# A fused two-block network: five FFN phases start on the unnormalised stream

## The chip, the cores and the metric

The kernel runs on one core of a Trainium2 chip, as one launch. The metric is the device time of that launch in microseconds (us). The core has five engines that matter here, each with a queue of its own that is worked off in order: TensorE (PE), VectorE (DVE), ScalarE (ACT), GpSimd (POOL) and SyncE (SP, which issues the weight loads). They are held together by semaphores alone.

## What is computed

A batch of one, 256 tokens, width 1024. Two networks of two layers each follow one another on the stream x. Cut to what matters:

```python
def rms_norm(x, g):
    return x * rsqrt(mean(x * x, axis=-1) + EPS) * g
def modulate(h, shift, scale):
    return h * (1 + scale) + shift

# first network, layers i = 0, 1 (nine vectors of 1024 from c_act @ ada_w[i] + ada_b[i])
h = modulate(rms_norm(x, ln_ffn1[i]), sh1, sc1)
x = x + 0.5 * g1 * swiglu(h, wg, wu, wd)          # phases F0, F2
h = modulate(rms_norm(x, ln_mix[i]), sh2, sc2)
x = x + g2 * mixer(h)                             # A (attention), G (spatial gating)
h = modulate(rms_norm(x, ln_ffn2[i]), sh3, sc3)
x = x + 0.5 * g3 * swiglu(h, wg, wu, wd)          # phases F1, F3
x = rms_norm(x, ln_out[i])

# second network, layers 0, 1 (six vectors each)
x = x + g1 * mixer(rmsnorm(x, norm_mix) * (1 + sc1) + sh1)     # H (HGRN2), N (sparse attention)
x = x + g2 * conv_ffn(rmsnorm(x, norm_ffn) * (1 + sc2) + sh2)  # C0, C1
# last: rmsnorm(x, final_norm)

swiglu(h, wg, wu, wd) = (silu(h @ wg) * (h @ wu)) @ wd          # hidden width 2816
conv_ffn: a, v = split(h @ w_up); a = three causal taps over the tokens + conv_b
          (silu(a) * v) @ w_down
```

## The kernel before

**Phases.** The order is F0, A, F1, F2, G, F3, H, C0, N, C1, then the last norm. The stream x lies in SBUF with the width on the partitions: eight blocks k of 128 channels, each 128 x 256 tokens. It is never turned around between phases.

**Slabs.** All weights stream from HBM in slabs of 128 x 2048 numbers of float32. Each slab is split for TensorE into a high part (`split_hi`, a cast on ScalarE, L1853) and a low part, raw minus high (`split_lo`, VectorE, L1986; at the border of two phases in two halves, L2001). A product with one slab is 48 matmuls of 256 columns: high x high, high x low and low x high, summed in PSUM (`three`, L1627 to L1629). TensorE waits for a slab's low part (`slab_ready`), and a split waits until TensorE has used the slab that lay in its buffer (`slab_used`). So the splits run two to four slabs ahead of TensorE, and where they stand in the ScalarE's and VectorE's queues is written out by hand.

**An FFN phase** with first slab b works on 11 chunks of 256 hidden channels. Chunk i takes three slabs: gate and up (`ups(i)` on TensorE, into PSUM `up`) and down (`down(i)`, into PSUM `dacc`). TensorE's order is ups(0), ups(1), down(0), ups(2), down(1), and then a loop over chunks 3 to 10. Between gate and down, ScalarE makes the Silu (L1909; in C0 and C1 first the tap part L1913, then two VectorE instructions for each half, L2141 and L2144, then the Silu L1919), VectorE the product with up (L2154), ScalarE its high part (L1924) and VectorE its low part (L2159). down(i) waits for the last of these.

**Modulation vectors.** In F0, F1, F2, F3 and C0 VectorE also multiplies tiles of the modulation matrix (`ada_tile`, 128 x 1024, L2021 and L2024), eight for one vector. TensorE then sums them over the partitions (`ada_sum`, L1721), the first time ahead of chunk 3. That sum stands in TensorE's queue, so a late eighth tile holds TensorE up. GpSimd issues the loads of these tiles.

**The norm at a phase's start** (`norm` on each engine). Behind the residual (L2119) ScalarE squares the eight blocks (L1871), GpSimd adds blocks 0 to 3 (`pre_add`, L1576), TensorE sums what is left over the partitions with a matrix of ones (`norm_sums`, five instructions in float32, recorded as ten, L1741) and then makes 24 dummy products whose result nobody reads (`keep_warm`, L1725 to L1729). ScalarE takes the root (L1877), VectorE the reciprocal (L2057), eight scalings x * a * (1/root) (L2060), ScalarE adds the shift and rounds to the high part of the operand (L1890, one per block) and VectorE makes the low part (L2064). TensorE's first product (`first_product`, L1652 and L1658) takes high parts block by block and then the low parts.

**Gained phases.** x = rms_norm(x, ln_out) behind F1 and F3 is not made before F2 and H, but folded into their norm: VectorE squares the plain x as well (`plain_squares`, L2111), GpSimd adds these eight too, TensorE sums them behind the first product (`gain_sum`), ScalarE takes the root (`row_kept`), and VectorE updates x itself (`gain_update`: a reciprocal and eight scalings), in F2 in halves around the slab b+3 and in H in its first two steps. In H GpSimd then builds masks, with fills and selects of 128 x 64 (L783 to L786).

Of the kernel before, what the change touches and what calls it, by code (L numbers as in the profile page):

```python
# [34 lines left out]
P = 128  # L35
# [65 lines left out]
def build(nc, T, out):  # L101
    phases = PHASES
    nslabs = sum(SLABS_OF.get(p, FFN_SLABS) for p in phases)
    with ExitStack() as ctx:
# [28 lines left out]
        work = sb("work", 12500)  # L133

# [6 lines left out]
        def op_k(t, k):  # L141
            return t[:, k * SEQ:(k + 1) * SEQ]

# [19 lines left out]
        table_col = small[:, 124:125]  # L163

# [5 lines left out]
        def bank(t, j):  # L170
            return t[:, j * 512:(j + 1) * 512]

# [13 lines left out]
            ada_step ada_summed mod_done x_turned squared squared_g presummed presummed_g sums_done sums_g_done  # L186
# [64 lines left out]
        gained = [phases[i + 1] for i, p in enumerate(phases) if p in OUT_COL]  # L251

# [41 lines left out]
        squares_g = view(4096, 6144)  # L294
# [150 lines left out]
        def pe_attention(pe, slab_ready, col_product, row_product, down_product, operand_stat, operand_mov, ada_sum, token_product):  # L445
# [76 lines left out]
        def act_attention(act, link, split_hi, split_hi_next, head_norm):  # L522
# [137 lines left out]
        def pe_gating(pe, slab_ready, col_product, row_product, down_product, operand_stat, operand_mov, ada_sum, token_product):  # L660
# [33 lines left out]
        def act_gating(act, link, split_hi, split_hi_next, head_norm):  # L694
# [82 lines left out]
        def hgrn_pool_masks(pool, link):  # L777
            pool.wait_ge(S["x_done"], x_before("H"))
# [28 lines left out]
        def pe_hgrn(pe, slab_ready, col_product, row_product, down_product, operand_stat, operand_mov, ada_sum, token_product):  # L807
            b = BASE["H"]
            for m in range(8):
                slab_ready(b + m)  # L810
                if m >= 6:
                    pe.wait_ge(S["sg_done"], 2 * (m - 5))
                col_product(b + m, ab_banks[m % 6], "H" if m == 0 else None)
            pe.wait_ge(S["sg_done"], 8)
# [67 lines left out]
        def act_hgrn(act, link, split_hi, split_hi_next, head_norm):  # L882
# [16 lines left out]
            for m in range(12):  # L899
                split_hi(b + m + 2)  # L900
                if 1 <= m <= 8:
                    take(m - 1)
                if m == 6:
# [42 lines left out]
        def dve_hgrn(dve, link, split_lo, ada_tile, mod_vector, residual, gain_update, head_norm):  # L946
# [155 lines left out]
        def pe_nsa(pe, slab_ready, col_product, row_product, down_product, operand_stat, operand_mov, ada_sum, token_product):  # L1102
# [111 lines left out]
        def act_nsa(act, link, split_hi, split_hi_next, head_norm):  # L1214
# [322 lines left out]
        def _(pool):  # L1537
# [733 lines left out]
```

## Time and profile before

| | us |
|---|---|
| three runs | 1977.41, 1980.89, 1980.24 |
| median | 1980.24 |
| the profiled execution | 1976.79 |
| its span | 1975.1 |

The profile is one execution. Over its span TensorE is busy for 1861.2 us (94%), VectorE for 1379.1 (70%), ScalarE for 859.1 (43%) and GpSimd for 263.5 (13%). The mean granted clock of TensorE is 0.957 of its full speed. TensorE's busy time counts the overlap of matmuls that follow each other as they are recorded, so its share says that it is the engine to watch, not that it never waits. Where it waits, a timeline row carries in brackets the idle time before it and what ended it. The page's other parts (DMA, 209 GB/s on the mean) do not bear on the change.

### The profile page before, as it was taken

What the parts mean: (1) busy time and instruction counts of PE and PEld (TensorE: products, weight loads), DVE (VectorE), ACT (ScalarE), POOL (GpSimd) and SP (SyncE); (2) the same over time, 40 slices, a digit from 0 to 9 for tenths busy, and PEclk for the clock granted to TensorE, in tenths of its full rate; (3) what the DMA queues carried; (4) which work ended last, traced back from release to release, by engine and by line L of the source; (5) the groups of instructions that cost most, each with busy time, mean ns of one, the idle gap of its engine ahead of it and who ended that gap; (6) DMA issues with size and microseconds to landing.
All of it is one profiled execution on the core that took longest, in us unless ns stands there. A gap on an engine that the chain in (4) does not pass through costs nothing.

```text
span 1975.1 us, 35516 instructions
## 1 busy us (share of the span) xinstructions
PE 1861.2 (94%) x14231; PEld 1786.2 (90%) x14231; DVE 1379.1 (70%) x1523; ACT 859.1 (43%) x1140; POOL 263.5 (13%) x429
## 2 busy tenths in 40 slices
PE   6999998799998999999999998779999998999998
PEld 6999996799998999988999987779999996689998
DVE  6677698576677866755677786757687856746555
ACT  3433454543334343444333454445344543645444
POOL 2311100011112111100111223720111110000000
PEclk9999998799999999988999998989999996999999
DMA  9988674168883988472888664035788792025551
GB/s 350 369 290 305 217 267 170 30 215 286 275 306 122 330 298 273 153 254 69 294 278 298 211 204 158 23 107 178 259 293 272 191 271 71 1 74 172 188 175 42
DMA packets 256950, 411.93 MB, mean 209 GB/s; under 512 B 22055, under 2 KB 200785, under 8 KB 256722
## 3 DMA queue, kind: packets, MB, share of 16 engines
q1 hardware_dynamic: 223914, 291.32, 45.3%
q0 software_dynamic: 32432, 119.04, 16.5%
q8 instruction: 70, 1.15, 0.2%
q14 instruction: 30, 0.25, 0.0%
q10 hardware_dynamic: 504, 0.18, 0.0%
HBM read 409.43 MB, written 2.63 MB: 209 GB/s over the span
## 4 chain that ended last, share of the span: by engine, by line
PE 80%; DVE 9%; ACT 3%; DMA 2%; issue 2%; POOL 2%; SPq 1%; DVEq 0%; ACTq 0%
PE up L1627 13%; PE up L1629 13%; PE up L1628 13%; PE dacc L1627 8%; PE dacc L1628 8%; PE dacc L1629 8%; PE dacc L1698 3%; PE misc L1721 3%; PE up L1652 2%; ACT hi L1853 1%; DVE lo L1986 1%; POOL work L1560 1%; DVE rstd_row L2057 1%; PE misc L1741 1%; DVE ada_acc L2024 1%
## 5 line engine op out<-in xcount | busy, mean ns | idle before, releaser
L1986 DVE TENSOR_TENSOR lo<-raw,hi 128x2048 fp32r<-128x2048 f32 (+1 forms) x256 | 581.0, 2271 | 332.3 <-ACT hi L1853 332.0
L1853 ACT CAST hi<-raw 128x2048 fp32r<-128x2048 f32 (+1 forms) x266 | 498.7, 1877 | 512.3 <-PE dacc L1629 253.1
L1627 PE MATMUL up<-operand_hi,hi 128*128 128x256 f32 x2176 | 621.1, 285 | 1.0 <-DVE work L2154 1.0
L1629 PE MATMUL up<-operand_hi,lo 128*128 128x256 f32 x2176 | 618.0, 284 | 0.0
L1628 PE MATMUL up<-operand_lo,hi 128*128 128x256 f32 x2176 | 618.0, 284 | 0.0
L1627 PEld LDWEIGHTS up<-operand_hi,hi 128*128 128x128 f32 x2176 | 419.9, 193 | 1.8 <-issue 1.7
L1628 PEld LDWEIGHTS up<-operand_lo,hi 128*128 128x128 f32 x2176 | 419.9, 193 | 0.6 <-issue 0.5
L1629 PEld LDWEIGHTS up<-operand_hi,lo 128*128 128x128 f32 x2176 | 419.7, 193 | 0.0
L1628 PE MATMUL dacc<-act_lo,hi 128*128 128x256 f32 x1056 | 298.8, 283 | 0.0
L1629 PE MATMUL dacc<-act_hi,lo 128*128 128x256 f32 x1056 | 298.4, 283 | 0.0
L1627 PE MATMUL dacc<-act_hi,hi 128*128 128x256 f32 x1056 | 296.5, 281 | 0.0
L2024 DVE SCALAR_TENSOR_TENSOR ada_acc<-ada,small,ada_acc 128x1024 f32<-128x1024 f32 x199 | 255.0, 1282 | 7.7 <-DMA ada<-in_ada_w_dram 3.5
L1423 POOL DMA_DIRECT2D ada<-in_ada_w_dram x224 | 118.9, 531 | 1001.1 <-DVE ada_acc L2024 611.6
L1627 PEld LDWEIGHTS dacc<-act_hi,hi 128*128 128x128 f32 x1056 | 200.8, 190 | 0.0
L1629 PEld LDWEIGHTS dacc<-act_hi,lo 128*128 128x128 f32 x1056 | 198.2, 188 | 0.0
L1628 PEld LDWEIGHTS dacc<-act_lo,hi 128*128 128x128 f32 x1056 | 197.9, 187 | 0.0
L1627 PE MATMUL dacc<-operand_hi,hi 128*128 128x256 f32 x464 | 136.4, 294 | 4.6 <-DVE operand_lo L758 2.2
L1628 PE MATMUL dacc<-operand_lo,hi 128*128 128x256 f32 x464 | 133.7, 288 | 0.0
L1629 PE MATMUL dacc<-operand_hi,lo 128*128 128x256 f32 x464 | 133.4, 288 | 0.0
L1576 POOL TENSOR_TENSOR work<-work 128x256 f32<-128x256 f32 x44 | 39.9, 908 | 617.7 <-ACT work L1871 615.9
L1909 ACT ACTIVATE work<-up 128x512 f32<-128x512 f32 x44 | 26.3, 598 | 183.0 <-PE up L1629 182.5
L1627 PEld LDWEIGHTS dacc<-operand_hi,hi 128*128 128x128 f32 x464 | 91.6, 197 | 6.9 <-DVE lo L1986 2.8
(364 smaller groups left out, 2481.7 us busy)
## 6 DMA issues: line engine op xcount, KB each, us to landing
ada<-in_ada_w_dram POOLq DMA_DIRECT2D x224, 512.0 KB, 5.9
raw<-in_ffn_wg_dram SPq DMA_DIRECT2D x88, 512.0 KB, 4.8
raw<-in_ffn_wu_dram SPq DMA_DIRECT2D x88, 512.0 KB, 5.3
raw<-in_ffn_wd_dram SPq DMA_DIRECT2D x88, 512.0 KB, 4.5
raw<-in_ffn_w_up_dram SPq DMA_DIRECT2D x88, 512.0 KB, 4.5
raw<-in_ffn_w_down_dram SPq DMA_DIRECT2D x46, 512.0 KB, 4.4
raw<-in_hg_w_in_dram SPq DMA_DIRECT2D x32, 512.0 KB, 5.0
raw<-in_attn_w_qkv_dram SPq DMA_DIRECT2D x24, 512.0 KB, 7.2
```

The lines of the kernel that those rows point to most:

```text
L1423: eng.dma_start(ada_place(m), ada_source(v, k) if source is None else source).then_inc((ada_first if v < 2 else ada_full)[m % ATILES], 16)
L1576: ins = pool.tensor_tensor(op_k(sq, 0), op_k(sq, 0), op_k(sq, k), ALU.add)
L1627: pe.matmul(o, stat[0], mov[0], start=start, stop=False, skip_group_check=True)
L1628: pe.matmul(o, stat[0], mov[1], start=False, stop=False, skip_group_check=True)
L1629: return pe.matmul(o, stat[1], mov[0], start=False, stop=stop, skip_group_check=True)
L1652: pe.matmul(dst[:, b * SEQ:(b + 1) * SEQ], sl[q][:, k * SEQ + b * P:k * SEQ + (b + 1) * P], op_k(operand_hi, k), start=(k == 0 and b == 0 ...
L1698: last = pe.matmul(bank(dacc, 2 * t + h), stat(part, kk, t), sl[q][:, kk * D + h * 512:kk * D + (h + 1) * 512], start=(start and kk == 0 a ...
L1721: last = pe.matmul(bank(misc, 1)[:, k:k + 1], acc_of(v)[:, k * P:(k + 1) * P], ones[:, 0:1], start=True, stop=True, skip_group_check=True)
L1853: last = act.copy(put(slab(hi, s, SPL)), take(slab(raw, s, RAW)))
L1909: act.activation(silu_sb, bank(up, 0), ACT.Silu).then_inc(S["silu_done"], 1)
L1986: last = dve.tensor_tensor(put(slab(lo, s, SPL)), take(slab(raw, s, RAW)), put(slab(hi, s, SPL)).bitcast(F32), ALU.subtract)
L2024: dve.scalar_tensor_tensor(acc, t, c, acc, ALU.mult, ALU.add).then_inc(S["ada_step"], 1)
```

## The change

All FFN phases but F0 are now in `raw_first` (F1, F2, F3, C0, C1). With a = gain * (1 + scale) for each channel, the operand of a product is x * a / root + shift. Since 1/root belongs to the token (the column), W @ (x*a) can be made first, multiplied by 1/root and the shift's product W @ shift added. That is done for the gate and the up product of chunk 0:

- ScalarE rounds x * a to `raw_hi` in pairs of blocks between the squares, behind a first instruction that puts two columns of the shift behind each block. VectorE makes the shift's rest and, among the residual's instructions, `raw_lo` = x * a - raw_hi. A block is 258 columns wide.
- TensorE makes `raw_products`: 32 matmuls with raw_hi, the sums (three instead of five, since GpSimd now adds blocks 0 to 5), 16 with raw_lo, and the whole up product, into four banks of `dacc`. The dummy products are gone in these phases. The products from chunk 1 on use the normed operand as before.
- VectorE copies the shift's column as a bias and multiplies with the root row (`first_scaled`), ScalarE's Silu takes the bias (`first_silu`; in C0 and C1 it makes the whole gate and then the tap part), and VectorE's `first_product` adds up's bias and multiplies. down(0), which writes into dacc, waits for `up_scaled`.
- The splits move: slab b+2 ahead of the root and the reciprocal, b+3 ahead of ScalarE's operand and behind VectorE's low parts, b+4 behind `first_silu` and `first_scaled` and ahead of the taps and the product.
- In F2 and H VectorE's eight plain squares are gone. GpSimd squares the plain blocks and adds them, 15 instructions. `gain_sum` stands behind ups(1) in F2 and behind the fourth product in H, the gain's root behind chunk 1 (H: step 5), and the update of x behind chunks 1 and 2 (H: steps 6 and 8). GpSimd's masks in H wait for the gain's sum. H keeps its norm otherwise.

```diff
 # POOL: pre_add
+top = 5 if name in raw_first else 3
+for k in range(1, top + 1):
+    ins = pool.tensor_tensor(op_k(squares, 0), op_k(squares, 0), op_k(squares, k), ALU.add)
+if name in gained:
+    pool.wait_ge(S["x_done"], x_before(name))
+    link(pool.tensor_tensor(gain_acc, op_k(x, 0), op_k(x, 0), ALU.mult))
+    for k in range(1, KB):
+        link(pool.tensor_tensor(gain_tmp, op_k(x, k), op_k(x, k), ALU.mult))
+        ins = pool.tensor_tensor(gain_acc, gain_acc, gain_tmp, ALU.add)
 # PE
+def raw_products(p):
+    slab_ready(b)
+    dst = [bank(dacc, q)[:, 0:RW] for q in range(4)]
+    for k in range(KB):
+        pe.wait_ge(S["raw_hi_done"], (KB + 1) * i + k + 2)
+        ... 4 matmuls of slab b (high, low; two halves) with raw_k(raw_hi, k)
+    norm_sums(p)
+    for k in range(KB):
+        pe.wait_ge(S["raw_lo_done"], KB * i + k + 1)
+        ... 2 matmuls of slab b's high part with raw_k(raw_lo, k)
+    slab_ready(b + 1)
+    ... three(...) for slab b + 1, 48 matmuls, into dst[2], dst[3]
-                ups(0)
+                if p in raw_first:
+                    raw_products(p)
+                else:
+                    ups(0)
                 ups(1)
+                if p in gained:
+                    gain_sum(p)
+                if p in raw_first:
+                    pe.wait_ge(S["up_scaled"], raw_first.index(p) + 1)
                 down(0, start=True)
-                if p != phases[0]:
+                if p != phases[0] and p not in raw_first:
                     norm(p)
 # ACT: norm
+for c in range(KB // 2):
+    for k in (2 * c, 2 * c + 1):
+        act.activation(raw_k(raw_hi, k)[:, 0:SEQ], op_k(x, k), ACT.Copy, scale=a_col[:, k:k + 1])
+    for k in (2 * c, 2 * c + 1):
+        act.activation(op_k(squares, k), op_k(x, k), ACT.Square, scale=...)
+if name in raw_first:
+    split_hi(b + 2)
 # ACT: ffn
+def first_silu():
+    act.wait_ge(S["gate_scaled"], n + 1)
+    for j in range(2):
+        act.activation(silu_sb[:, o], gate_first[:, o], ACT.Silu, bias=first_bias[:, j:j + 1])
+        (conv: gate_first = Identity(gate_first + bias), then the tap part into silu_sb)
+first_silu()
+split_hi(b + 4)
 # DVE
+def raw_rest(ks):
+    dve.wait_ge(S["raw_hi_done"], (KB + 1) * raw_first.index(q) + k + 2)
+    dve.scalar_tensor_tensor(raw_lo_k, op_k(x, k), a_col[:, k:k + 1], raw_hi_k, ALU.mult, ALU.subtract)
+def first_scaled():
+    for m, dst in enumerate((gate_first, up_first)):
+        dve.wait_ge(slab_used, b + m + 1)
+        dve.tensor_copy(first_bias[:, 2 * m:2 * m + 2], first_banks(m, SEQ, 1))
+        dve.tensor_tensor(dst, first_banks(m, 0, SEQ), row, ALU.mult)
+def first_product():
+    dve.wait_ge(S["silu_done"], u + 1)
+    ins = dve.scalar_tensor_tensor(act32[:, o], up_first[:, o], first_bias[:, 2 + j:3 + j], silu_sb[:, o],
+                                   ALU.add, ALU.mult)
 # DVE: ffn
-                split_lo(b + 2)
                 if p in gained:
-                    gain_update(p, range(4))
-                taps(0)
-                split_lo(b + 3)
-                    gain_update(p, range(4, KB))
-                product(b + 1, 0)
+                    split_lo(b + 3)
+                    first_scaled()
+                    split_lo(b + 4)
+                    taps(0)
+                    first_product()
                 hidden_lo(0)
-                iteration(1, 0, v, 0, (0, 2, 2))
-                iteration(2, 0, v, 4, (2, 1, 1))
+                iteration(1, 0, v, 0, (0, 2, 2), ahead=p in raw_first)
+                if p in gained:
+                    gain_update(p, range(4))
+                iteration(2, 0, v, 4, (2, 1, 1))
+                if p in gained:
+                    gain_update(p, range(4, KB))
```

VectorE at the start of F1, the program before (`lo`, `hi`: a slab's parts; `work` is shared by squares, scaled x and activations):

```order
L2119 SCALAR_TENSOR_TENSOR x<-dacc,modcol,x 128x256 x2
L2001 TENSOR_TENSOR lo<-raw,hi 128x1024
L2119 SCALAR_TENSOR_TENSOR x<-dacc,modcol,x 128x256 x6
L2001 TENSOR_TENSOR lo<-raw,hi 128x1024
L2057 RECIPROCAL rstd_row<-rstd_row 128x256
L2060 SCALAR_TENSOR_TENSOR work<-x,small,rstd_row 128x256 x8
L2064 SCALAR_TENSOR_TENSOR operand_lo<-work,modcol,operand_hi 128x256 x8
L1986 TENSOR_TENSOR lo<-raw,hi 128x2048 x2
L2154 TENSOR_TENSOR work<-work,up 128x512
L2159 TENSOR_TENSOR act_lo<-work,act_hi 128x512
L1986 TENSOR_TENSOR lo<-raw,hi 128x2048 x2
```

The same place in the program after; `work_r` holds raw_hi and raw_lo:

```order
L2114 TENSOR_TENSOR lo<-raw,hi 128x1024
L2099 TENSOR_TENSOR lo<-raw,hi 128x2048
L2172 RECIPROCAL rstd_row<-rstd_row 128x256
L2175 SCALAR_TENSOR_TENSOR work<-x,small,rstd_row 128x256 x8
L2179 SCALAR_TENSOR_TENSOR operand_lo<-work,modcol,operand_hi 128x256 x8
L2099 TENSOR_TENSOR lo<-raw,hi 128x2048
L2265 COPY small<-dacc 128x2
L2266 TENSOR_TENSOR work<-dacc,rstd_row 128x512
L2265 COPY small<-dacc 128x2
L2266 TENSOR_TENSOR work<-dacc,rstd_row 128x512
L2099 TENSOR_TENSOR lo<-raw,hi 128x2048
L2278 SCALAR_TENSOR_TENSOR work<-work,small 128x256 x2
```

Ahead of this piece the eight rests stand among the residual's instructions. Here one slab's low part has come ahead of the reciprocal, and the third slab's low part stands between the scaling of gate and up (reading `dacc`) and the product.

ScalarE at the start of F1 before:

```order
L1871 ACTIVATE work<-x 128x256 x8
L1877 ACTIVATE rstd_row<-misc,small 128x256
L1890 ACTIVATE operand_hi<-work,modcol 128x256 x8
L1853 CAST hi<-raw 128x2048
L1909 ACT_TABLE_LOAD
L1909 ACTIVATE work<-up 128x512
L1853 CAST hi<-raw 128x2048
L1924 CAST act_hi<-work 128x512
```

And after:

```order
L1944 ACTIVATE work_r<-x,small 128x256 x2
L1948 ACTIVATE work<-x 128x256 x2
L1919 CAST hi<-raw 128x2048
L1956 ACTIVATE rstd_row<-misc,small 128x256
L1919 CAST hi<-raw 128x2048
L1971 ACTIVATE operand_hi<-work,modcol 128x256 x8
L1995 ACT_TABLE_LOAD
L1995 ACTIVATE work<-work,small 128x256 x2
L1919 CAST hi<-raw 128x2048
L2030 CAST act_hi<-work 128x512
```

The squares are in pairs with the raw parts, two casts have come ahead of the operand's eight instructions, and the third cast stands behind the Silu and ahead of the product's high part.

GpSimd at the start of F2 after, where before ten additions (L1576) stood in one run and nothing read x:

```order
L1449 DMA ada<-in_ada_w_dram 128x1024 x4
L1599 TENSOR_TENSOR work<-work 128x256 x5
L1605 TENSOR_TENSOR work<-x 128x256
L1607 TENSOR_TENSOR work<-x 128x256
L1608 TENSOR_TENSOR work<-work 128x256
L1607 TENSOR_TENSOR work<-x 128x256
L1608 TENSOR_TENSOR work<-work 128x256
```

The five additions are those of the scaled squares; the rest is the squaring and adding of the plain blocks, in a chain through one accumulator.

## Rows read from the trace of the kernel before

**Rows 1.** The page's part 4: shares of the chain that ended last, by engine.

```profile
PE 80%; DVE 9%; ACT 3%; DMA 2%; issue 2%; POOL 2%; SPq 1%; DVEq 0%; ACTq 0%
```

**Rows 2.** TensorE's timeline, start of F1: start us, us, line, operation, xcount [idle <-releaser].

```profile
399.26 2.32 PE L1741 MATMUL misc<-work,ones 128*128 128x256 f32 x10
401.42 2.84 PE L1729 MATMUL up<-ident,ones 128*128 128x128 f32 x24
405.16 0.36 PE L1652 MATMUL up<-operand_hi,hi 128*128 128x256 f32 x1 [0.90 <-ACT operand_hi L1890]
...
409.06 2.08 PE L1658 MATMUL up<-operand_lo,hi 128*128 128x256 f32 x16
```

**Rows 3.** VectorE's timeline, start of F1.

```profile
400.26 1.22 DVE L2001 TENSOR_TENSOR lo<-raw,hi 128x1024 fp32r<-128x1024 f32 x1
402.20 1.75 DVE L2057 RECIPROCAL rstd_row<-rstd_row 128x256 f32<-128x256 f32 x1 [0.73 <-ACT rstd_row L1877]
403.99 3.26 DVE L2060 SCALAR_TENSOR_TENSOR work<-x,small,rstd_row 128x256 f32<-128x256 f32 x8
407.16 3.25 DVE L2064 SCALAR_TENSOR_TENSOR operand_lo<-work,modcol,operand_hi 128x256 fp32r<-128x256 f32 x8
...
418.31 0.69 DVE L2159 TENSOR_TENSOR act_lo<-work,act_hi 128x512 fp32r<-128x512 f32 x1 [0.69 <-ACT act_hi L1924]
```

**Rows 4.** ScalarE's timeline, F1.

```profile
411.67 1.89 ACT L1853 CAST hi<-raw 128x2048 fp32r<-128x2048 f32 x1
417.66 0.62 ACT L1924 CAST act_hi<-work 128x512 fp32r<-128x512 f32 x1 [4.09 <-DVE work L2154]
```

**Rows 5.** TensorE's timeline at five later places (F1, F2, F2, C0, C0).

```profile
451.95 1.94 PE L1721 MATMUL misc<-ones,ada_acc 128*128 128x1 f32 x16 [0.50 <-DVE ada_acc L2024]
...
606.82 2.67 PE L1741 MATMUL misc<-work,ones 128*128 128x256 f32 x10 [0.24 <-ACT work L1871]
...
665.85 1.94 PE L1721 MATMUL misc<-ones,ada_acc 128*128 128x1 f32 x16 [0.50 <-DVE ada_acc L2024]
...
1345.97 2.32 PE L1741 MATMUL misc<-work,ones 128*128 128x256 f32 x10
...
1400.36 3.21 PE L1721 MATMUL misc<-ones,ada_acc 128*128 128x1 f32 x16 [2.20 <-DVE ada_acc L2024]
```

**Rows 6.** The taps of C0, ScalarE and VectorE.

```profile
1357.89 1.02 ACT L1913 ACTIVATE work<-up,cols 128x256 f32<-128x256 f32 x2 [1.56 <-PE up L1658]
...
1359.24 0.49 DVE L2141 SCALAR_TENSOR_TENSOR work<-up,cols,work 128x255 f32<-128x255 f32 x1
...
1361.07 2.28 DVE L1986 TENSOR_TENSOR lo<-raw,hi 128x2048 fp32r<-128x2048 f32 x1
```

**Rows 7.** VectorE and GpSimd side by side, F2 (605 to 616) and H (1181 to 1189).

```profile
605.46 9.03 POOL L1576 TENSOR_TENSOR work<-work 128x256 f32<-128x256 f32 x9 [0.48 <-ACT work L1871]
606.53 0.75 DVE L2111 TENSOR_TENSOR work<-x 128x256 f32<-128x256 f32 x2
609.56 3.54 DVE L2111 TENSOR_TENSOR work<-x 128x256 f32<-128x256 f32 x4
...
1181.80 1.27 DVE L2024 SCALAR_TENSOR_TENSOR ada_acc<-ada,small,ada_acc 128x1024 f32<-128x1024 f32 x1
1182.36 0.87 POOL L784 TENSOR_SCALAR_AFFINE_SELECT work<-work 128x64 f32<-128x64 f32 x1
1189.14 0.24 POOL L784 TENSOR_SCALAR_AFFINE_SELECT work<-work 128x64 f32<-128x64 f32 x1
```

**Rows 8.** TensorE's timeline in H; last row windows: busy by engine, clock, DMA, GB/s.

```profile
1139.00 0.55 PE L1652 MATMUL up<-operand_hi,hi 128*128 128x256 f32 x1 [3.81 <-ACT operand_hi L1890]
...
1154.24 0.39 PE L1627 MATMUL dacc<-operand_hi,hi 128*128 128x256 f32 x1 [0.54 <-DVE lo L1986]
...
1166.76 0.39 PE L1627 MATMUL dacc<-operand_hi,hi 128*128 128x256 f32 x1 [0.27 <-DVE lo L1986]
...
1140.00:1145.00 5.00, 5.00 (x26) 5.00 (x26) 4.74 (x15) 1.65 (x5) 0.00 (x0) 0.52 0.01 3
```

More of the change, by code:

```diff
@@ L251, in build @@
         gained = [phases[i + 1] for i, p in enumerate(phases) if p in OUT_COL]
+        raw_first = [p for p in FFNS if p != phases[0]]
         def x_count(p):
@@ L1733, in norm_sums @@
                 n = norm_list.index(name)
-                order = list(range(KB)) if n == 0 else [4, 5, 0, 6, 7]
+                order = list(range(KB)) if n == 0 else [0, 6, 7] if name in raw_first else [4, 5, 0, 6, 7]
                 for k in order:
@@ L1750, in gain_sum @@
                 pe.wait_ge(S["presummed_g"], gained.index(p) + 1)
[L1751 removed]
+                pe.matmul(misc[:, SEQ:2 * SEQ], ones[:, :], gain_acc, start=True,
                           stop=True, skip_group_check=True).then_inc(S["sums_g_done"], 1)
@@ L1899, in ffn @@
                 conv = p[0] == "C"
+                def first_silu():
+                    n = raw_first.index(p)
+                    u = count_up(p, 0)
+                    act.wait_ge(S["gate_scaled"], n + 1)
+                    if u:
+                        act.wait_ge(S["prod_done"], u)
+                    for j in range(2):
+                        o = slice(j * SEQ, (j + 1) * SEQ)
+                        if not conv:
+                            ins = act.activation(silu_sb[:, o], gate_first[:, o], ACT.Silu, bias=first_bias[:, j:j + 1])
+                            if j:
+                                ins.then_inc(S["silu_done"], 1)
+                            continue
+                        act.activation(gate_first[:, o], gate_first[:, o], ACT.Identity,
+                                       bias=first_bias[:, j:j + 1]).then_inc(S["gate_full"], 1)
+                    for j in range(2 if conv else 0):
+                        o = slice(j * SEQ, (j + 1) * SEQ)
+                        act.wait_ge(S["gate_full"], 2 * (n - raw_first.index("C0")) + 2)
+                        act.activation(silu_sb[:, o], gate_first[:, o], ACT.Identity, scale=tap(p, 2, 0, j),
+                                       bias=tap(p, 3, 0, j)).then_inc(S["tap_a"], 1)
                 def silu(s, i, it=0):
@@ L1924, in hidden_hi, with iteration @@
                     act.copy(act_hi[:, o:o + 2 * SEQ], act32).then_inc(S["acthi_done"], 1)
-                def iteration(i, it=0):
+                def iteration(i, it=0, ahead=False):
                     a = b + 3 * i - 1
-                    split_hi(a + 2, it)
+                    if not ahead:
+                        split_hi(a + 2, it)
                     silu(a, i, it)
@@ L2170, in some @@
                         return k + n
-                    split_lo(a + 2, it)
+                    if not ahead:
+                        split_lo(a + 2, it)
                     if summed is not None:
```

171 lines of the change are left out of this document (120 added, 51 removed).

## The prediction

> **What bounds the kernel now.** I began with the chain that ended last: TensorE holds 80% of it, so the kernel is paid for by TensorE's own work and by its few pauses [rows 1]. Then I read TensorE's timeline where one FFN phase (F1) takes over from the mixer before it. After the last product of the mixer TensorE makes the ten records of the square sums (2.16 us from start to start), 24 dummy products of the warm-up (2.84 us), idles 0.90 us and starts F1's first product at 405.16: 5.90 us after 399.26. From 405.16 to 409.06 there are 32 matmuls, so one takes 0.12 us and a product of 48 takes 5.76 us [rows 2]. Four products on, at 405.16 + 23.04 = 428.2, the first down product begins with no wait. Third, VectorE and ScalarE in the same stretch: their list of jobs there is nearly gapless [rows 3, 4]. Fourth, the later places where TensorE waits: the sum of the modulation vector (L1721) begins when VectorE's eighth ada tile is done, at 451.95 in F1 after 0.50 us of idling, at 665.85 in F2, and in C0 at 1400.36 after 2.20 us [rows 5]. So two or three products into a phase VectorE, not TensorE, already sets the time. What the change gives TensorE has to pass there.
>
> **TensorE's part.** Gone are the warm-up and two of five sums. What is left before F1's third product, from 399.26: 32 matmuls on the raw stream 3.9, six sum records 1.3, 16 on its rests 1.9, the second product 5.8, so 412.1. Before it was 405.16 + 11.52 = 416.7. TensorE alone would win 4.6 us in each of F1, F3, C0 and C1. That a matmul of 258 columns costs as much as one of 256 is an assumption (two columns more of 256 would be 1 ns; the other end, twice the time, is a rival).
>
> **VectorE's part in F1, step by step.** It adds eight rests (x times gain minus the high part) at 0.40 each: eight such instructions take 407.16 - 403.99 = 3.17 [rows 3]. Before, half of its slab work ended at 400.26 + 1.22 = 401.5. Now x blocks 2 to 7 (2.4), eight rests (3.2) and the half slab (1.1) follow 397.2 (400.26 less six residual instructions of 0.40 and 0.66 of waiting for TensorE): 403.9, and three meetings with GpSimd's adds (below) make it 405.3. Then, each from its row: a whole slab's low part 2.2 [rows 6] (407.5), reciprocal 1.7 (409.2), eight scalings 3.2, eight low parts 3.2 (415.6), slab b+3 2.2 (417.8), bias copy and gate times the root row 0.75 (418.6; the nearest row is the 128x512 one of 0.69). ScalarE: two Silu of 256, 0.85 (419.4), high part of slab b+4 1.85 [rows 4] (421.3). VectorE: its low part 2.25 (423.5), the two instructions of the product 0.8, ScalarE's act_hi 0.6, VectorE's act_lo 0.7 with hand-overs (425.75). TensorE, due at 423.8, begins the first down product at 425.9 instead of 428.2: 2.3 won of 4.6, since one serial chain of VectorE and ScalarE is now last. New here is that slab b+4's split stands behind the Silu in ScalarE's queue and so behind the gate's scaling.
> From there to the eighth ada tile VectorE has: slab b+5 (waiting for ScalarE to 427.4) to 429.6, then four slabs 8.8, seven ada tiles 8.0, two products and two low parts of the activations 2.5 and the last tile 1.2, 20.6 in all with nothing idle: 450.2. The sum starts at 450.35 against 451.95. **F1: -1.6. F3, the same code in the same pattern: -1.6.**
>
> **C0 and C1** have the taps. The gate is made whole (0.9 for two), then two tap instructions on ScalarE (0.9) come ahead of slab b+4, four on VectorE (1361.07 - 1359.24 = 1.8) [rows 6] and a Silu (0.6, as ScalarE's act_hi of that width [rows 4]) behind it; 0.85 of Silu falls away. That is 3.3 later than F1: in F1's clock act_lo ends at 429.05 and the down product starts at 429.3, 1.1 later than before. **C1: +1.1** (no ada tiles, TensorE keeps that lag). In C0 VectorE still has 20.6, one slab's 2.2 and two pairs of taps of 1.8, together 26.4, and waits 0.3 for ScalarE's taps: 429.05 + 26.7 = 455.75. C0's sums start at 1345.97 [rows 5] against 399.26, 946.7 later, so the last tile ends at 1402.5 and the sum starts at 1402.65 against 1400.36: **C0: +2.3**.
>
> **F2 and GpSimd.** VectorE loses eight plain squares, GpSimd gets 15 instructions (mult and add) in a row, just while VectorE scales. Two plain squares of VectorE take 0.75, but four of them take 3.54 beside GpSimd's adds: 0.87 each instead of 0.33, the two engines taking turns [rows 7]. So one GpSimd instruction costs VectorE 0.54. That scalar_tensor_tensor behaves the same is shown once: a GpSimd select of 0.24 took 0.87 at 1182.36, ending 0.15 after VectorE's L2024 ended at 1183.07 [rows 7]. Bounds: 0 and 15 x 0.54 = 8.1. I take 7.0, since two of the 15 fall beside the reciprocal, which reads one tensor. Carrying F1's 51.1 us from last product to sum over to F2 (last product out at 606.4, since the sums there start at 606.82 after a wait [rows 5]) gives 657.5. Reciprocal and half the gain update are now ahead of the last tile (1.75 + 4 x 0.40): 660.85. Plus 7.0: 667.8 against 665.85. **F2: +1.95.** ScalarE's two more table loads lie in its idle time.
> The Trainium skill, SBUF — State Buffer, "Who interferes with whom", says that a VectorE instruction with two SBUF inputs contends with a GpSimd instruction that reads SBUF, and that the one which issues first holds the pair for its whole length. The trace agrees, 0.87 against 0.33. By this rule every scaling and rest waits, and the sum is the one above; without it the sum is the first rival's.
>
> **H** keeps its norm. Without the last four squares (3.5 us) the first product can start at 1135.8 instead of 1139.00. But from 1134.9 the 16 scalings and low parts (6.3 us) take turns with some ten GpSimd instructions still left (10 x 0.54, 5.6 with the odd end), so the last low part comes at 1146.8 and product one ends at 1147.5. Before, it ended at the same time: 1154.24 less the 0.54 waited, a second product of 5.76 and the gain sum of 0.43 is 1147.5. It had run at a granted clock of 0.52, the 1.2 GHz level, over 1140 to 1145, after 3.81 us of idling [rows 8]. What is left is the gain update (5 us of VectorE), which moves to where VectorE waits for the masks: TensorE's waits of 0.54 and then 1166.76 - 1154.24 - 11.52 = 1.0 go [rows 8]. **H: -1.5.**
>
> **Sum:** -1.6 - 1.6 + 1.95 + 2.3 + 1.1 - 1.5 = +0.65. The profiled execution took 1976.79 (span 1975.1), so 1977.4 for it. The median of the three runs, 1980.24, is 3.45 above it; 1980.24 + 0.65 is 1980.9, and I predict 1981.0.
>
> **Rivals.**
> 1. GpSimd's turns cost VectorE nothing. For: only tensor_tensor rows show VectorE held up, never a scalar_tensor_tensor. Against: the select held by L2024. Then F1 and F3 -2.5 each, C0 +1.5, C1 +0.2, F2 660.8 - 665.85 = -5.0, H -7.5 (product one 3.6 earlier and 2.4 of low clock saved): -15.8, so 1964.5. Chance 0.20, with the cases half way.
> 2. TensorE's own path decides everywhere, as the change means it: 4 x 4.6, and 3.81 idle plus 2.4 of low clock in F2 and in H, about -31, so 1949. Against it stand the gapless rows 3. Chance 0.05.
> 3. Slower: TensorE's clock falls in F2 and H, where it now has 0.48 us of matmuls for each 0.93 of VectorE over 8 us and then waits 2.0 and 1.7. For: it fell after 3.81 idle at both places. Against: no single gap is as long any more. In H low clock cost 26 x 0.09 = 2.4; twice that with the products behind it in both phases: about +5, so 1986. It decides once the lag outlasts VectorE's own. Chance 0.19. The Trainium skill, TensorE: Matmul & The Clock Gate, "What's actually happening", says that the throttled state is the default and activity releases it; no row here shows what half activity does.
> 4. The 258-column matmuls cost double: 96 x 0.12 = 11.5 a phase, less the 2 to 5 waited anyway: five times about 8, so 2020. No row shows one. Chance 0.06.
> The likeliest case has 0.50, its own range 1977 to 1985.
>
> **How the numbers follow.** About 0.2% (4 us) is what a measurement of this kernel tells from no change. Faster: rivals 1 and 2 (of 0.25, 0.24) and 0.09 of the likeliest: 0.33. Slower: rival 3 (0.16), rival 4 (0.06) and 0.05: 0.27. Within: 0.40. The range reaches down to near rival 1 and up past rival 3: 1966 to 1988.
>
> **What would show it.** In F1: raw products from 399.3 with no gap, first down product at 426 after a wait of 2 on act_lo, the ada sum at 450.3. In F2: scalings 0.9 apart, TensorE waiting between each, sum at 667.8. In C0 a wait over 5 before the first down product. It is wrong if scalings beside GpSimd stay at 0.40, if the matmuls of 258 columns are not 0.12 apart, or if the clock is low in F2 or H.

## The result and the profile after

The changed kernel is slower: the ratio of its runs to those of the kernel before is 1.0045, with a 95% interval of 1.0028 to 1.0062, about 8.9 us. Over twenty runs each the medians are 1984.97 us after and 1974.33 us before (the three runs shown ahead of the prediction, with a median of 1980.24, lay high). The profiled execution after took 1986.27 us (span 1983.7, granted clock 0.950), against 1976.79 before.

The page's chain that ended last, after (shares by engine):

```profile
PE 74%; DVE 16%; ACT 4%; issue 3%; SPq 1%; DMA 1%; POOL 1%; DVEq 0%; ACTq 0%
```

TensorE fell from 80% to 74% of the chain and VectorE rose from 9% to 16% [rows 1]. The view of TensorE's waits says where (engine, line, waited for: us in all, times, longest). Before:

```profile
PE up L1652 <- ACT operand_hi L1890: 13.7, 8, 3.8
...
PE misc L1721 <- DVE ada_acc L2024: 4.6, 5, 2.2
```

After:

```profile
PE dacc L1659 <- DVE act_lo L2307: 16.5, 5, 5.6
...
PE misc L1780 <- DVE ada_acc L2137: 8.6, 5, 4.6
```

The waits of 13.7 us before the first products have lost their place at the top; five waits of 16.5 us before the first down products stand there instead, one in each changed phase. The sums of the modulation vectors wait for 4.0 us more.

TensorE's timeline in F1, after (answers to [rows 2, 5]):

```profile
404.45 1.46 PE L1800 MATMUL misc<-work,ones 128*128 128x256 f32 x6
405.56 2.26 PE L1712 MATMUL dacc<-work_r,hi 128*128 128x258 f32 x16
...
424.79 0.28 PE L1661 MATMUL up<-operand_hi,lo 128*128 128x256 f32 x1
426.94 0.36 PE L1659 MATMUL dacc<-act_hi,hi 128*128 128x256 f32 x1 [1.87 <-DVE act_lo L2307]
...
452.19 1.05 PE L1780 MATMUL misc<-ones,ada_acc 128*128 128x1 f32 x8 [0.50 <-DVE ada_acc L2137]
```

VectorE and ScalarE there (answers to [rows 3, 4]):

```profile
422.34 2.29 DVE L2099 TENSOR_TENSOR lo<-raw,hi 128x2048 fp32r<-128x2048 f32 x1 [2.11 <-ACT hi L1919]
424.55 0.87 DVE L2278 SCALAR_TENSOR_TENSOR work<-work,small 128x256 f32<-128x256 f32 x2
426.11 0.69 DVE L2307 TENSOR_TENSOR act_lo<-work,act_hi 128x512 fp32r<-128x512 f32 x1 [0.68 <-ACT act_hi L2030]
```

```profile
419.60 0.91 ACT L1995 ACTIVATE work<-work,small 128x256 f32<-128x256 f32 x2 [4.19 <-DVE work L2266]
420.42 1.89 ACT L1919 CAST hi<-raw 128x2048 fp32r<-128x2048 f32 x1
```

Mixer A ended 1.34 us later in this execution, so in the clock of the profile before TensorE was due at 423.7, started the down product at 425.6 and the ada sum at 450.85. TensorE's work is done early, and it waits 1.87 us for the activation's low part. ScalarE idles for 4.19 us before its Silu and has slab b+4's cast behind it; VectorE then waits 2.11 us for that cast.

TensorE in F2, C0 and C1, after (answers to [rows 5]):

```profile
666.46 1.64 PE L1780 MATMUL misc<-ones,ada_acc 128*128 128x1 f32 x8 [4.65 <-DVE ada_acc L2137]
...
1373.79 0.55 PE L1659 MATMUL dacc<-act_hi,hi 128*128 128x256 f32 x1 [5.61 <-DVE act_lo L2307]
...
1400.75 1.44 PE L1780 MATMUL misc<-ones,ada_acc 128*128 128x1 f32 x6 [2.41 <-DVE ada_acc L2137]
...
1804.41 0.55 PE L1659 MATMUL dacc<-act_hi,hi 128*128 128x256 f32 x1 [5.61 <-DVE act_lo L2307]
```

And the windows behind four of these waits (columns as in [rows 8]: stretch, length, busy us and count of PE, PEld, DVE, ACT, POOL, then the granted clock, DMA share, GB/s):

```profile
428.00:431.00 3.00, 3.00 (x16) 3.00 (x15) 2.61 (x2) 2.15 (x2) 0.00 (x0) 0.50 0.24 97
...
667.50:673.00 5.50, 5.50 (x26) 5.50 (x27) 4.71 (x6) 0.00 (x0) 0.64 (x2) 0.50 1.07 377
...
1373.80:1376.70 2.90, 2.90 (x13) 2.90 (x14) 2.76 (x5) 2.71 (x4) 0.00 (x0) 0.50 0.00 0
...
1804.50:1810.00 5.50, 5.50 (x26) 5.50 (x27) 5.43 (x7) 4.79 (x4) 0.00 (x0) 0.50 0.01 3
```

In each the clock is 0.50, the 1.2 GHz level, after TensorE has idled: in F2 and C1 26 matmuls in 5.5 us, where 46 would fit at 0.12 us each. So the gap of 5.61 us before C1's first down product cost about 2.4 us more behind it. In C0 the same gap of 5.61 us was followed by 2.9 us at 0.50. The window of 667.5 to 673 before, where TensorE had idled for only 0.50 us:

```profile
667.50:673.00 5.50, 5.50 (x47) 5.50 (x47) 4.13 (x4) 0.00 (x0) 1.05 (x2) 1.00 0.96 323
```

The second profile of the kernel before (before_again) has the same wait of 0.50 us at the same sum, and there the clock did fall behind it:

```profile
668.60:672.00 3.40, 3.40 (x18) 3.40 (x17) 3.07 (x4) 0.00 (x0) 0.53 (x1) 0.50 0.90 295
```

The length of each phase, from the end of the last weight product of the phase ahead to that of its own, worked out from the traces; the last three columns are differences from the first profile before:

| phase | before | before, second profile | after | after, second profile |
|---|---|---|---|---|
| A (mixer) | 156.79 | +0.18 | +1.90 | +0.65 |
| F1 | 207.15 | -1.49 | -1.09 | -1.65 |
| F2 | 212.41 | +1.57 | +3.48 | +3.26 |
| G (mixer) | 103.46 | 0.00 | +0.29 | +0.28 |
| F3 | 207.16 | 0.00 | -1.09 | -1.10 |
| H (mixer) | 216.53 | +0.13 | -5.19 | -2.67 |
| C0 | 210.47 | -0.02 | +2.59 | +2.65 |
| N (mixer) | 213.46 | -0.13 | +4.10 | +3.18 |
| C1 | 195.98 | 0.00 | +3.69 | +2.73 |

The second profiles are the runs before_again and changed_again below. The six phases F1, F2, F3, H, C0 and C1 sum to +2.4 and +3.2 us over the first profile before; N alone adds another 3 to 4.

A stretch of half clock behind the first ada sum is there in one profile and missing in another of the same kernel, and it moves a phase by about 1.5 us. So the start of that sum, counted from the phase's start, is the steadier measure. From the two profiles before to the two after, in us: F1 52.53 and 52.53 to 51.42 and 50.88; F2 59.27 and 59.35 to 59.64 and 59.62; F3 52.53 and 52.53 to 51.44 and 51.44; C0 54.22 and 54.22 to 56.87 and 56.87. Against the second profile before, F1's length is +0.4 and -0.2, and F2's +1.9 and +1.7.

The mixers and the last norm are touched in one place as well. ScalarE's loop over pairs of blocks holds for every norm, also where there are no raw parts, and it asks for both blocks of a pair before it squares the first:

```diff
-for k in range(KB):
-    act.wait_ge(S["x_done"], x_before(name) - KB + k + 1)
-    act.activation(op_k(squares, k), ...)
+for c in range(KB // 2):
+    for k in (2 * c, 2 * c + 1):
+        act.wait_ge(S["x_done"], x_before(name) - KB + k + 1)
+        ...
+    for k in (2 * c, 2 * c + 1):
+        act.activation(op_k(squares, k), ...)
```

VectorE's reciprocal in G, whose phase starts at 818.98 before and at 822.71 after:

```profile
821.91 1.75 DVE L2057 RECIPROCAL rstd_row<-rstd_row 128x256 f32<-128x256 f32 x1 [0.88 <-ACT rstd_row L1877]
...
825.93 1.75 DVE L2172 RECIPROCAL rstd_row<-rstd_row 128x256 f32<-128x256 f32 x1 [1.17 <-ACT rstd_row L1956]
```

It starts 0.29 us later in the phase, which is all of G's +0.29. In A and N it starts 0.45 us later (2.77 to 3.22), and in the last norm 0.4 to 0.7, in all nine profiles of changed kernels: 1.6 to 1.9 us of the slowdown that the sums over the six phases do not hold. No run takes the pairing alone back, so the cause of this part is read from the code and the rows.

### The profile page after: what moved, and what is told of

It is laid out like the page before. It is cut to its first block, busy times and chain, and to the rows that moved or that the text cites. A ratio compares the mean times of both kernels' runs of the same rounds, so it can differ in the third digit from the quotient of the medians.

```text
span 1983.7 us, 35382 instructions
## 1 busy us (share of the span) xinstructions
PE 1860.2 (94%) x14091; PEld 1780.1 (90%) x14091; DVE 1405.6 (71%) x1577; ACT 880.1 (44%) x1195; POOL 274.3 (14%) x455
## 4 chain that ended last, share of the span: by engine, by line
PE 74%; DVE 16%; ACT 4%; issue 3%; SPq 1%; DMA 1%; POOL 1%; DVEq 0%; ACTq 0%
PE up L1659 11%; PE up L1660 11%; PE up L1661 11%; PE dacc L1659 8%; PE dacc L1660 8%; PE dacc L1661 8%; PE dacc L1757 3%; PE misc L1780 3%; DVE lo L2099 2%; DVE work L2175 2%; ACT hi L1919 1%; DVE work_r L2229 1%; DVE operand_lo L2179 1%; DVE ada_acc L2137 1%; DVE x L2239 1%
## 5 line engine op out<-in xcount | busy, mean ns | idle before, releaser
L1659 PE MATMUL up<-operand_hi,hi 128*128 128x256 f32 x2016 | 576.1, 286 | 1.8 <-DVE lo L2099 1.8
L1660 PE MATMUL up<-operand_lo,hi 128*128 128x256 f32 x2016 | 573.4, 284 | 0.0
L1661 PE MATMUL up<-operand_hi,lo 128*128 128x256 f32 x2016 | 573.4, 284 | 0.0
L1659 PEld LDWEIGHTS up<-operand_hi,hi 128*128 128x128 f32 x2016 | 390.0, 193 | 2.5 <-DVE lo L2099 2.0
L1660 PEld LDWEIGHTS up<-operand_lo,hi 128*128 128x128 f32 x2016 | 389.8, 193 | 0.5 <-issue 0.5
L1661 PEld LDWEIGHTS up<-operand_hi,lo 128*128 128x128 f32 x2016 | 389.7, 193 | 0.0
L1659 PE MATMUL dacc<-act_hi,hi 128*128 128x256 f32 x1056 | 300.6, 285 | 16.5 <-DVE act_lo L2307 16.5
L1599 POOL TENSOR_TENSOR work<-work 128x256 f32<-128x256 f32 x40 | 30.3, 759 | 632.5 <-ACT work L1948 630.9
```

What stands on the lines that cost most here:

```text
L1599: ins = pool.tensor_tensor(op_k(squares, 0), op_k(squares, 0), op_k(squares, k), ALU.add)
L1659: pe.matmul(o, stat[0], mov[0], start=start, stop=False, skip_group_check=True)
L1660: pe.matmul(o, stat[0], mov[1], start=False, stop=False, skip_group_check=True)
L1661: return pe.matmul(o, stat[1], mov[0], start=False, stop=stop, skip_group_check=True)
```

## The experiments

**changed_again**, no edit. 

> The changed kernel once more, unedited, for a second profile. Theory: the phases that the change touches repeat within 0.5 us (F1 and F3 -1.1 against before, F2 +3.5, C0 +2.6, C1 +3.7), while the mixers A (+1.9) and N (+4.1), whose instructions are the same, move by some us from one execution to the next with the stretches of half clock. Rival (the change does lengthen the mixers): A and N show +1.9 and +4.1 again.

Measured: ratio 1.0047 (1.0024 to 1.0070), a span of 1986.8 us. F1, F3, C0 and F2 repeat within 0.6, C1 within 1.0 (0.5 was expected: F1 with 0.56 and C1 with 0.96 miss it), and H moved by 2.5. Mixer A moved back to +0.65, N stayed at +3.18. The same wait of 1.87 us before F1's down product was followed by a full clock this time (window view):

```profile
429.60:433.00 3.40, 3.37 (x28) 3.40 (x29) 1.92 (x1) 3.25 (x2) 0.00 (x0) 1.00 0.54 217
```

So the clock's answer to a wait of that length is not fixed. Of the two expectations on the mixers one half holds each: A varies, N does not go back.

**before_again**, the kernel before. 

> The kernel before, unedited, for a second profile. If the mixers vary by themselves, A and N differ by a microsecond or more from 156.8 and 213.5 us of the first profile while the FFN phases F1, F3 (207.15) repeat within 0.5; if the change lengthens N, N is again near 213.5, against 216.4 to 217.6 of four changed kernels.

Measured: one run of 1978.40 us. A is 156.97, N 213.33, F1 205.66 (1.5 shorter, where the stretch of half clock behind its ada sum is missing), F3 207.16. N at 213.3 and 213.5 in two profiles of the kernel before, against 216.4 to 217.6 in six of the others, speaks for a real cost in N, of which the pairs of squares explain 0.45. But N was 207.9 in dummies, 207.4 in combined_gate_early and 213.8 in taps_ahead, and the granted clock over N goes with it: 0.89 in both profiles before, 0.87 to 0.88 in the long ones, 0.92 and 0.93 in the short ones. What sets N's clock stays open.

**cast_ahead**, slab b+4's cast before the first Silu:

```diff
 if p in raw_first:
-    first_silu()
     split_hi(b + 4)
+    first_silu()
```

> The changed kernel with one edit: ScalarE casts slab b+4 before the first Silu instead of behind it. Theory (a serial chain through VectorE and ScalarE is last): the cast fits into the 4.2 to 5.5 us in which ScalarE waits for the scaled gate, VectorE's low part of b+4 no longer waits 2.1 us (3.2 in C0 and C1), TensorE's wait before the first down product falls from 1.87 us to about 0 in F1 and F3, from 1.53 to 0 in F2 and from 5.61 to about 2.3 in C0 and C1, and the half clock behind it goes or shortens. F1 and F3 2 to 3 us shorter each, F2 2, C0 and C1 3 each: 12 us below the changed kernel, a ratio to the kernel before of about 0.999. Rival (what VectorE has to do up to the eighth ada tile sets the time, whatever stands before the first down product): C1 alone gains 3, the others under 1 each.

Measured: ratio 0.9971 (0.9951 to 0.9992), so 0.76% or 15 us below the changed kernel, give or take 6 by the two intervals. TensorE starts F1's down product without a wait, C0's after 2.30 us (TensorE's timeline in C0, then VectorE's in F1):

```profile
1370.60 0.55 PE L1659 MATMUL dacc<-act_hi,hi 128*128 128x256 f32 x1 [2.30 <-DVE act_lo L2307]
```

```profile
421.88 2.29 DVE L2099 TENSOR_TENSOR lo<-raw,hi 128x2048 fp32r<-128x2048 f32 x1
424.08 0.88 DVE L2278 SCALAR_TENSOR_TENSOR work<-work,small 128x256 f32<-128x256 f32 x2
425.64 0.69 DVE L2307 TENSOR_TENSOR act_lo<-work,act_hi 128x512 fp32r<-128x512 f32 x1 [0.69 <-ACT act_hi L2030]
```

VectorE's 2.11 us of waiting for the cast is gone. Against changed_again F1 is 0.6 us shorter, F2 1.0, F3 1.2, C0 3.3 and C1 3.4. That is 9.5 us in these five; the rest of the 15 they do not show. The theory's size holds for C0 and C1. In F1 and F2 the ada sum starts 2.2 us earlier in the phase than in changed_again (48.68 for 50.88, 57.45 for 59.62) and in F3 2.8 (48.68 for 51.44), so VectorE's list up to it did get shorter and the rival's reason is not borne out. But TensorE waits for the sum all the same (1.34 us in F1, 4.41 in F2), and the half clock behind it is longer: 6.8 us for 3.4 in F1, and in F2 9.0 (below) for 6.3. That takes the larger part of the gain, so the phases end near the rival's "under 1 each".

```profile
664.90:673.90 9.00, 9.00 (x42) 9.00 (x43) 5.79 (x8) 0.00 (x0) 1.58 (x3) 0.50 1.03 372
```

**dummies**, in TensorE's queue ahead of the down product, in all but F2:

```diff
     pe.wait_ge(S["up_scaled"], raw_first.index(p) + 1)
+    if p not in gained:
+        keep_warm(bank(misc, 0), 22 if p[0] == "C" else 7)
 down(0, start=True)
```

> The changed kernel with dummy products in TensorE's wait before the first down product: 7 in F1 and F3, 22 in C0 and C1, none in F2. Theory (the half clock behind that wait comes from the idling): the matmuls of the first down product run 0.12 us apart from the start, the stretches of 3.2 us (F1, F3), 2.9 us (C0) and 5.7 us (C1) at half clock vanish, which gives back 1.2 to 1.6 us in F1, F3 and C0 and 2.5 in C1, where nothing else is last, and less in F1, F3 and C0, where the eighth ada tile is last: 3 to 6 us in all. Rival (the clock falls there for another reason, or the time is set by VectorE): no change, or later by the dummies that overshoot.

Measured: ratio 1.0017 (0.9995 to 1.0039), 6 us below the changed kernel, by intervals that overlap. The down product starts at the same place in the phase, but at full clock (windows in F1, C0 and C1):

```profile
427.00:431.00 4.00, 4.00 (x36) 4.00 (x35) 2.88 (x2) 2.90 (x2) 0.00 (x0) 1.00 0.36 140
1373.00:1376.00 3.00, 2.89 (x24) 2.92 (x25) 2.73 (x5) 2.82 (x4) 0.00 (x0) 1.00 0.02 5
1803.00:1811.00 8.00, 8.00 (x69) 8.00 (x69) 5.41 (x6) 3.44 (x4) 0.00 (x0) 1.00 0.78 261
```

C1, where nothing of VectorE is due behind it, is 197.12 against 198.71 and 199.67. C0 gave nothing back (213.14): its ada sum waited 3.70 us instead of 2.41. F1 is 205.52 against 206.06 and 205.50, and F3, which has no half clock at all in this profile, 204.02 against 206.07 and 206.06. With dummies in the wait the clock stays up in all four phases, so it is the idling that makes it fall; what the full clock gives is kept where VectorE is not last later (C1), lost in C0, and mixed in F1 and F3. Some of the 6 us may be N's, which was short in this profile.

**conv_as_before**, C0 and C1 with the old start:

```diff
-raw_first = [p for p in FFNS if p != phases[0]]
+raw_first = [p for p in FFNS if p != phases[0] and p[0] != "C"]
```

> The changed kernel with C0 and C1 as before the change (norm, warm-up and first products on the normed operand, taps ahead of slab b+3's low part). The phases C0 and C1 cost 2.6 and 3.7 us more than before in the one trace. Theory: they go back, 210.5 and 196.0 us, and the kernel is 6 us below the changed one, a ratio to before of about 1.001. Rival (their cost is only the clock's chance of that execution): under 2 us.

Measured: ratio 0.9998 (0.9978 to 1.0018), 10 us below the changed kernel, with an interval of several us on that difference. C0 is 209.30 (1.2 less than in the kernel before) and C1 196.42, 3.8 and 2.3 us less than in changed_again. The change costs about 6 us in the two phases with taps, and what is left of it is a draw.

**no_gpsimd_squares**: GpSimd squares two plain blocks and adds nothing.

```diff
 link(pool.tensor_tensor(gain_acc, op_k(x, 0), op_k(x, 0), ALU.mult))
-for k in range(1, KB):
-    link(pool.tensor_tensor(gain_tmp, op_k(x, k), op_k(x, k), ALU.mult))
-    ins = pool.tensor_tensor(gain_acc, gain_acc, gain_tmp, ALU.add)
-    if k < KB - 1:
-        link(ins)
+ins = pool.tensor_tensor(gain_acc, op_k(x, 1), op_k(x, 1), ALU.mult)
```

> The changed kernel without fourteen of GpSimd's fifteen instructions on the plain stream in F2 and in H (only one block is squared; so the gain's root is taken of wrong sums). Theory (each of them holds VectorE up): F2's eight scalings take 3.26 us instead of 6.33, the last four rests 2.2 instead of 3.4, the ada sum in F2 starts about 5 us earlier and its wait falls from 4.65 to near 0, F2 is 4.5 us shorter; in H scalings and low parts take 3.26 and 3.25 instead of 6.33 and 4.56, and H is 3 to 4 us shorter: 8 us below the changed kernel, a ratio to before of about 1.000. Rival (VectorE's rows are long there for another reason, such as waits for ScalarE's high parts): the rows stay at 6.33 and the time at 1.0047.

Two instructions are left, not one, so thirteen are gone, and the gain's root is taken of wrong sums. Measured: ratio 1.0019 (1.0000 to 1.0038), 5.5 us below the changed kernel. VectorE in F2, first in the changed kernel, then here:

```profile
609.22 3.37 DVE L2229 SCALAR_TENSOR_TENSOR work_r<-x,small,work_r 128x256 fp32r<-128x256 f32 x4
...
618.58 6.33 DVE L2175 SCALAR_TENSOR_TENSOR work<-x,small,rstd_row 128x256 f32<-128x256 f32 x8
624.84 3.24 DVE L2179 SCALAR_TENSOR_TENSOR operand_lo<-work,modcol,operand_hi 128x256 fp32r<-128x256 f32 x8
```

```profile
607.82 2.89 DVE L2225 SCALAR_TENSOR_TENSOR work_r<-x,small,work_r 128x256 fp32r<-128x256 f32 x4
...
615.74 3.26 DVE L2171 SCALAR_TENSOR_TENSOR work<-x,small,rstd_row 128x256 f32<-128x256 f32 x8
618.92 3.25 DVE L2175 SCALAR_TENSOR_TENSOR operand_lo<-work,modcol,operand_hi 128x256 fp32r<-128x256 f32 x8
```

GpSimd in the changed kernel beside the scalings, two of eight such rows:

```profile
618.93 0.80 POOL L1608 TENSOR_TENSOR work<-work 128x256 f32<-128x256 f32 x1
619.81 0.68 POOL L1607 TENSOR_TENSOR work<-x 128x256 f32<-128x256 f32 x1
```

Eight scalings cost 3.07 us more beside GpSimd, and the low parts, made after GpSimd had ended, are undisturbed. F2 is 211.35, 4.3 us less than in changed_again. The ada sum starts 4.5 us earlier in the phase, yet its wait is 4.64 as before, since TensorE is earlier too: I had expected it near 0, and forgot that TensorE's own third product waits for the same scalings (the first down product too starts 4.5 us earlier in the phase, 27.05 for 31.57). In H the fourth product starts 4.2 us earlier in the phase than in the changed kernel, but H as a whole is 211.20, against 211.35 in the first profile after and 213.87 in the second: of the 3 to 4 us expected there, 0.2 and 2.7.

**combined_late_gain**: cast_ahead, nine dummies in C0 and C1, and in F2

```diff
-if p in gained:
-    gain_update(p, range(4))
 iteration(2, 0, v, 4, (2, 1, 1))
 if p in gained:
+    gain_update(p, range(4))
     gain_update(p, range(4, KB))
```

> The changed kernel with slab b+4's cast ahead of the first Silu, in F2 the whole gain update behind chunk 2 instead of its first half between chunks 1 and 2, and nine dummy products in TensorE's 2.3 us wait before the first down product of C0 and C1. Against the run with the cast alone (F2 214.7, C0 209.8, C1 195.3 us, ratio 0.9971): theory, VectorE's list up to the eighth ada tile sets F2, so 3.35 us less of it brings F2's ada sum 3.35 us forward, wait 4.4 to about 1, F2 211.5; C1 gives back 1.4 of half clock, C0 nothing: about 4.5 us, ratio 0.995. Rival (the update only moves its 5 us of VectorE to the next thing that TensorE waits for): F2 stays at 214 to 215.

Measured: ratio 0.9937 (0.9913 to 0.9961). TensorE at F2's ada sum, and VectorE there:

```profile
661.65 0.71 PE L1780 MATMUL misc<-ones,ada_acc 128*128 128x1 f32 x5 [1.01 <-DVE ada_acc L2139]
```

```profile
660.24 1.28 DVE L2139 SCALAR_TENSOR_TENSOR ada_acc<-ada,small,ada_acc 128x1024 f32<-128x1024 f32 x1
661.43 1.74 DVE L2195 RECIPROCAL gain_row<-gain_row 128x256 f32<-128x256 f32 x1
663.21 3.26 DVE L2197 SCALAR_TENSOR_TENSOR x<-x,cols,gain_row 128x256 f32<-128x256 f32 x8
```

The wait fell from 4.41 to 1.01, the 3.35 us of the update that had stood ahead. F2 is 208.71, 6.0 us below cast_ahead: more than the 3.35, since the clock was low for 9.0 us behind the long wait (shown above) and for 3.4 behind the short one, which is worth another 2.8. F3, where nothing was edited, is 1.5 shorter too, with 3.4 us less of half clock. C1 gave 1.5 back, C0 nothing, both as expected.

**combined_gate_early**: the gate's scaling right behind the reciprocal, two dummies.

```diff
 link(dve.reciprocal(rstd_row[:, :], rstd_row[:, :]))
+if name in raw_first:
+    first_scaled(name, 0)
```

> The kernel of combined_late_gain with the gate's bias copy and scaling right behind the reciprocal, ahead of the eight scalings of the operand (up's stay where they were), and two dummy products instead of nine. Theory (the serial chain gate, Silu or taps, product, high, low part is last before the first down product): in C0 and C1 the taps start 1.6 us or more earlier and the wait of 2.3 falls to 0.7 or less, C1 1.5 us shorter; F1 and F3 unchanged within 0.5, since the operand's first block comes still ahead of TensorE; ratio 0.994. Rival (the operand's scalings come late by 0.75 us and TensorE's third product waits): F1 and F3 0.5 to 1 us longer each.

Measured: ratio 0.9936 (0.9913 to 0.9960), the same. C0 and C1 are 209.82 and 193.81, unchanged to 0.02 us: a miss of the theory. TensorE waits 0.3 for slab b+3's low part. F1 was 1.6 us shorter, with 3.4 us at half clock behind its ada sum instead of 6.8, though the sum starts at the same place (48.67) and the first down product 0.56 later, as the rival said. The chain of the Silu was made earlier, but VectorE stood without a gap from the reciprocal to the taps, and the same instructions in another order end at the same time.

**taps_ahead**: the same with four dummies, and

```diff
-split_lo(b + 4)
 taps(0)
+split_lo(b + 4)
 first_product()
```

> The kernel of combined_gate_early with the four tap instructions of VectorE ahead of slab b+4's low part in C0 and C1 (and four dummy products instead of two). In both combined kernels the first down product of C0 and C1 started 24.7 us after the same mark, with VectorE gapless but for 1.4 us behind the taps, where it waits for the Silu (0.70) and for act_hi (0.68). Theory (VectorE's work, not the gate's lateness, is last there): the split fills the first of these gaps, the down product starts 0.7 us earlier, C1 0.7 us shorter, C0 0 to 0.7, the other phases as they were, ratio 0.993. Rival (the Silu's chain on ScalarE is last): no change at the down product.

Measured: ratio 0.9922 (0.9897 to 0.9947), the lowest, though its interval overlaps that of the two before it: about 15 us below the kernel before and 24 below the changed one. VectorE in C0:

```profile
1353.12 0.48 DVE L2294 SCALAR_TENSOR_TENSOR work<-work,cols 128x254 f32<-128x254 f32 x1
1353.52 2.29 DVE L2101 TENSOR_TENSOR lo<-raw,hi 128x2048 fp32r<-128x2048 f32 x1
1355.72 0.88 DVE L2280 SCALAR_TENSOR_TENSOR work<-work,small 128x256 f32<-128x256 f32 x2
```

The split fills the gap of 0.70 us behind the taps. The down product starts 0.78 earlier, C1 is 0.79 us shorter and C0 0.85, as the theory said. F1, which was to stay, is 1.5 shorter, without half clock behind its sum.

## Why the prediction held in its range and missed in its size

I forecast +0.65 us, no change that can be told, and gave slower by over 0.2% a chance of 0.27. It was slower by 0.45%. The time, 1984.97, lies in the range of 1966 to 1988, and even in the likeliest case's own 1977 to 1985, but that is luck in part: both are built on 1980.24, the median of three runs before, and the median of twenty is 1974.33. Moved down by these 5.9 us the range would have ended at 1982.1, and the time would lie above it. The likeliest case, no change, was wrong, and the clock was low in F2, which the prediction itself names as a sign against it. The step that failed is the price of TensorE's new and longer waits: their idle time was in the sum, the half clock behind them was put at nothing.

- **TensorE's part and F1, F3.** Right. In the clock of before: TensorE due at 423.8, measured 423.7; down product 425.9, measured 425.6; ada sum 450.35, measured 450.85. F3's sum starts 1.1 us earlier in the phase and F1's 1.1 and 1.65, for -1.6; F1's length says less, since before_again's F1 is as short as those after. The 258 columns cost nothing: the 48 matmuls from 407.66 to 413.41 in F1 are 0.12 us apart, and in the groups by line the median of a matmul is 282 to 283 ns with 256 and with 258 columns. That rules out rival 4.
- **C0 and C1.** The steps were right and a term was missing. Down product 1.1 later than before: measured 1.08 in both. C0 +2.3: measured +2.6. C1 +1.1: measured +3.7 and +2.7. I had the wait of over 5 us in the text and did not price the half clock behind it, in C1 26 matmuls in 5.5 us. In C0, where VectorE is last later, it cost little. I looked for the low clock in F2 and H (rival 3), not behind this wait. dummies shows that it comes from the idling; cast_ahead shows what the queue's order costs.
- **F2 and GpSimd.** The mechanism was right, with two errors of opposite sign. GpSimd held VectorE up, 0.38 us for each scaling: its price was 7.0 us in my sum and 4.5 by experiment for thirteen of the fifteen instructions (without them the ada sum starts at 661.7 in the clock of before, for my 660.85). The ada sum was so only 0.4 us later than before, where I had +1.95. But TensorE now waited 4.65 us for it, and the clock was at 0.50 for at least 5.5 us behind, where it had been 1.00 in the first profile before and low for 3.4 us in the second. F2 came out at +3.5 and +3.3 against the first and at +1.9 and +1.7 against the second, so that its forecast length was near by two errors that cancel. Rival 1 (GpSimd's turns cost nothing) has fallen, and rival 3 held in F2, at the ada sum instead of the scalings.
- **H.** -1.5 forecast, -5.2 and -2.7 measured. At the fourth product it was -3.1 and -3.0: the first product started 2.9 earlier, at full clock, the scalings took 0.79 us each instead of the 0.93 that I took, and the three waits went as said.
- **What was not in the sum.** The pairs of squares in A, G, N and the last norm, 1.6 to 1.9 us, which the prediction did not see in the diff. And N, +4.1 and +3.2 with these 0.45. Together with A it is over half of the slowdown in the first profile. TensorE's first long wait in N, for a slab's low part behind a load from HBM, grew from 0.99 (0.59) to 2.21 (1.81) us, and a lower clock goes with the rest. It was 1.79 in conv_as_before too, so C0's new start is not its cause. The cause is open; no experiment took it away on purpose.

The sum of the six phases, +0.65, was measured as +2.4 and +3.2. Of the difference C1 is 1.6 to 2.6, F2 1.3 to 1.5 and H gives 1.2 to 3.7 back.

## What to carry to other kernels

When work is taken off the engine that bounds a kernel, write out the list of the engine that feeds it, up to the next wait, and see what stands in its queue ahead of the piece that is now last. Here one cast ahead of a Silu instead of behind it was worth about 15 us by the runs and 9.5 in the phases' own lengths, as much as the change lost or more. See also what a rewritten loop does where the new case does not apply: a wait for two blocks instead of one cost every other norm 0.3 to 0.45 us. Price a new wait of TensorE twice: once as idle time, and once as the stretch at half clock that may follow. Where an engine has no gap, putting its instructions in another order changes nothing, but putting one into a gap does.

## What the hardware showed

- A VectorE scalar_tensor_tensor with two inputs in SBUF, 128 x 256, takes 0.40 us alone and 0.79 beside a GpSimd tensor_tensor of the same size, as the two take turns (F2 in the changed kernel and in no_gpsimd_squares).
- After waits of 4.65 and 5.61 us TensorE ran at 0.50 of its clock for 5.5 us and more in F2 and C1, after the same 5.61 us in C0 for 2.9. After the same 1.87 us in F1 it did so for 3.4 us in one profile and not at all in another, and after the same 0.50 us in F2 not at all in one profile of the kernel before and for 3.4 us in the other.
- A mixer with the same instructions took from 207.4 to 217.6 us in eleven executions, with its granted clock between 0.93 and 0.87. A single profile tells nothing of a change of 3 us in such a stretch; the FFN phases repeat within 1.6.
